# RMS norms of the second block: the next GEMM on x times gain, with rstd rows multiplied into its results

## The chip, the cores and the metric

One core of a Trainium2 chip runs the kernel. The metric is the device time of one execution, in microseconds. Its engines run side by side and meet only at semaphores: TensorE (PE) for matmuls, VectorE (DVE) and ScalarE (ACT) for elementwise work, GpSimd (POOL), and SyncE (SP), which here only issues DMAs.

## What is computed

The reference is two transformer-like blocks on x of 512 tokens by 1024 features, in float32. The change touches the second one. What matters of it:

```python
h = rmsnorm(x, g_mix)                       # x * rsqrt(mean(x*x) + eps) * gain
proj = h @ w_in                             # 11 parts of 1024 columns
xc, gb, gc, q, k, v, g_sw, gate_a, gate_r = split(proj)
u = gc * xc
conv = three taps over the tokens of u      # each feature for itself
y_a = (gb * conv) @ w_a_out
...                                         # retention over q, k, v -> y_r
x = x + (sigmoid(gate_a) * y_a + sigmoid(gate_r) * y_r) @ w_o
h2 = rmsnorm(x, g_ffn)
x = x + (silu(h2 @ w_ff_gate) * (h2 @ w_ff_up)) @ w_ff_down
return rmsnorm(x, g_final)
```

The rstd of a token multiplies a whole column of the transposed h, so `(x * gain * rstd) @ w` is `(x * gain) @ w` with each token's results times its rstd. For u = gc * xc that is rstd squared.

## The kernel before

Everything is kept transposed: 128 features on the partitions, the 512 tokens along the row, 8 such k-tiles for 1024 features. A GEMM is made of units. A unit is 128 output features: the weight slab of 128 x 1024 is loaded by SP (`load`, four slots), split on ACT into `w_hi` (`act_convert`, L380) and on DVE into the rest `w_lo` (`dve_convert`, L385), two units ahead (`AHEAD = 2`). `pe_unit` (L368) then runs three passes of 8 matmuls: w_hi by the operand's hi, w_lo by its hi, w_hi by its lo. ACT takes the result out of PSUM (`act_out`, L392). The order on each engine is that of the program, one stream for each.

The stages of the second half, in order: output projection of block one (8 units, `U_WO`), convolution (24 units, `U_CONV`: the three columns xc, gc, gb of eight tiles, one turn t for each tile), `U_YA` (16), retention's q, k, v (32), gates (24), `U_YR` (16), `U_O` (8), feed-forward (`U_FF`, 44 units, gate and up of 22 tiles), `U_DOWN` (24). Most of them are hardware loops (`Fori`) of a few turns.

A norm stands between `U_WO` and `U_CONV`, and another between `U_O` and `U_FF`. In each of them: `residual` (L1187, L1197) adds x and sums the squares that `out_and_square` makes on ACT (L784); `norm_sums` on PE (L1669) sums them over the partitions; DVE makes the mean (`norm_ms`, L1201); POOL the power of -0.5 (L579); `rows_bc` on PE (L1449) lays rstd along the rows in PSUM bank 5; `norm` on DVE makes t = x * gain * rstd for eight tiles (L1208); `round_norm` on ACT rounds them to `g_hi` (or `f_hi`, L789); DVE makes the rest `g_lo` (`f_lo`, L1212). Only then is the operand of the next GEMM there. Behind the first norm DVE also computes the retention's log decay, some thirty operations on 8 columns (L1222 to L1248), with one Exp on ACT (L798) in between. In the convolution, DVE multiplies xc by gc, applies three taps (L1263, L1265, L1268), multiplies by gb (L1273); ACT rounds to `a_hi` (L808), DVE makes `a_lo` (L1275).

Of the kernel before, what the change touches and what calls it, by code (L numbers as in the profile page):

```python
# [25 lines left out]
F32 = mybir.dt.float32  # L26
# [131 lines left out]
def hybrid_block(nc, x, c, w_ada, b_ada, norm_gain, w_in, b_nsa_gate, q_gain_a, k_gain_a, sinks,  # L158
# [7 lines left out]
    with ExitStack() as stack:  # L166
# [15 lines left out]
        def const(name, shape, dt=F32):  # L182
# [97 lines left out]
        ret = sb("ret", [P, 16, S], R + 48)  # L280
        ret_hi = sb("ret_hi", [P, 16, S], R + 48, F32R)
# [29 lines left out]
        m_hi = sb("m_hi", [P, KT, S], R, F32R)  # L311
        m_lo = sb("m_lo", [P, KT, S], R + 16, F32R)
# [3 lines left out]
        t_f = sb("t_f", [P, KT, S], R + 48)  # L316
# [11 lines left out]
        raw_in2 = [sem(f"raw_in2_{s}") for s in range(SLOTS)]  # L328
# [4 lines left out]
                 "tab_in consts csilu_done col_t col_done x_tr x_ev sumsq_done line_mm line_ev "  # L333
# [12 lines left out]
        nrm = {n: sem(n) for n in ("x_done xsq_done ss_done nst_mm ms_done rs_done nbc_mm t_done h_done l_done").split()}  # L346
# [9 lines left out]
        def pe_unit(pe, it, per, u, per_o, o, mov_hi, mov_lo, kts=KT, k0=0, first=True, last=True,  # L356
                    hi_sem=None, lo_sem=None, base=0):
# [6 lines left out]
            for n, (w, mov, ready) in enumerate(passes):  # L364
                for k in range(kts):
                    if ready is not None:
                        pe.wait_ge(ready, base + k0 + k + 1)
                    mm = pe.matmul(bank, w[:, slot, k], mov[:, k0 + k],  # L368
                                   start=first and n == 0 and k == 0,
                                   stop=last and n == 2 and k == kts - 1)  # L370
            mm.then_inc(unit_done, 1)

        def act_convert(act, it, per, u, kts=KT):
            slot = u % SLOTS
            act.wait_ge(raw_in[slot], at(it, 4 * per, 16 * (u // SLOTS + 1)))
            if u < U_PAIRED:
                act.wait_ge(raw_in2[slot], at(it, 4 * per, 16 * (u // SLOTS + 1)))
# [22 lines left out]
        def tile_of(t, it, per, n):  # L400
# [3 lines left out]
            return t[:, bass.ds(it * per + n, 1)].rearrange("p a n -> p (a n)")  # L404

# [18 lines left out]
        def _(sp):  # L424
# [17 lines left out]
            def load_pair(u, dst, dst2, src, src2):  # L442
# [4 lines left out]
                sp.dma_start(dst2, src2).then_inc(raw_in2[u % SLOTS], 16)  # L447
# [30 lines left out]
            with sp.Fori(0, 2) as it:  # L478
                for k in range(4):
                    load(it, 4, U_WO + k, w_out_v[:, :, wide(it * 512 + k * P)])  # L480
            with sp.Fori(0, 2) as it:
                for t in range(4):
                    for n, off in enumerate((0, 2048, 1024)):
                        load(it, 12, U_CONV + 3 * t + n, w_in2_v[:, :, wide(it * 512 + off + t * P)])
# [23 lines left out]
            with sp.Fori(0, 2) as it:  # L508
                for k in range(4):
                    load(it, 4, U_O + k, w_o_v[:, :, wide(it * 512 + k * P)])  # L510
            with sp.Fori(0, FT // 2) as it:
                for t in range(2):
                    load(it, 4, U_FF + 2 * t, w_g_v[:, :, wide(it * 256 + t * P)])
                    load(it, 4, U_FF + 2 * t + 1, w_u_v[:, :, wide(it * 256 + t * P)])
# [13 lines left out]
        def _(pool):  # L528
# [93 lines left out]
            pool.wait_ge(nrm["t_done"], KT)  # L622
# [37 lines left out]
        def _(act):  # L660
# [29 lines left out]
            with act.Fori(0, 2) as it:  # L690
                for k in range(8, 12):
                    act_convert(act, it, 4, k + AHEAD)
                    act_out(act, it, 4, k, tile_of(proj, it, 4, k), k, ACT.Copy)

            def square(t):
# [6 lines left out]
            for n in range(16, 24):  # L702
# [17 lines left out]
                if n < 19:  # L720
                    for t in range(*NORM_GROUPS[n - 16]):
                        square(t)
# [55 lines left out]
            def out_and_square(it, per, u, per_o, o, q, t, scale):  # L778

                act_out(act, it, per, u, t[:, o % 2], o, ACT.Copy, scale)  # L780
                count = at(it, per_o, q * KT + o - NORM_O[q] + 1)
                apart(act, it)
                act.wait_ge(nrm["x_done"], count)
                a.activation(t[:, 2 + o % 2], tile_of(x_t, it, per_o, o - NORM_O[q]), ACT.Square).then_inc(nrm["xsq_done"], 1)  # L784

            def round_norm(q, dst, t):
                for k in range(KT):
                    act.wait_ge(nrm["t_done"], q * KT + k + 1)
                    a.activation(dst[:, k], t[:, k], ACT.Copy).then_inc(nrm["h_done"], 1)  # L789

            with act.Fori(0, 2) as it:
                for k in range(4):
# [1051 lines left out]
```

## Time and profile before

| | |
|---|---|
| time, median of 3 runs | 1593.28 us (1589.33, 1593.28, 1594.75) |
| span of the profiled execution, first to last instruction | 1585.1 us (its own whole time is not recorded; the median is 8.2 us above the span) |
| PE matmul busy | 1515.8 us, 96% |
| DVE busy | 704.2 us, 44% |
| ACT busy | 589.0 us, 37% |
| POOL busy | 92.0 us, 6% |
| mean granted PE clock | 0.973 of full speed |
| DMA | 147.87 MB, mean 93 GB/s |

How to read it: the busy time of PE is an average over stages, and a busy PE is not always PE at full clock. A timeline row gives start, duration, engine, line, operation, tile written and tiles read, and in brackets how long the engine had been idle and what ended it. Matmuls overlap, so the end of a row is a little later than the start of the next; the distance between two starts is the time that counts.

### The profile page before, as it was taken

The page shows a single profiled execution, that of the slowest core. Times are in us where ns is not written, and L with a number is a line of the kernel's source. Part 1 is how long each engine was busy: PE and PEld are TensorE (multiplying, and loading weights), DVE is VectorE, ACT ScalarE, POOL GpSimd, SP SyncE. Part 2 cuts the span into 40 slices and gives each one's busy share as a digit, 9 for nine tenths or more (in the row PEclk, how much of TensorE's full clock was granted, in tenths as well). Part 3 has the DMA queues.
Part 4 walks back from the last instruction along what each step waited for, and adds up shares of the span by engine and source line. Part 5 has one row for each costly group of instructions (what it writes and reads, how often), then busy time and mean ns, then how long its engine had stood idle before and what let it go on. Part 6 is the DMA issues. An engine that isn't in the chain of part 4 may idle for free.

```text
span 1585.1 us, 20029 instructions
## 1 busy us (share of the span) xinstructions
PE 1515.8 (96%) x7068; PEld 1247.0 (79%) x7068; DVE 704.2 (44%) x1078; ACT 589.0 (37%) x955; POOL 92.0 (6%) x97
## 2 busy tenths in 40 slices
PE   7799998998989999999999999999998999999997
PEld 4578886887768888887787878887876888888886
DVE  4443256764465442344453524454445333333332
ACT  5232335653433334333333344443333333332321
POOL 5100500000000000000000023210000000000000
PEclk9799899998989999999999999999998999999999
DMA  9963320000333333331121213325232333333321
GB/s 328 328 135 95 106 60 9 1 2 14 89 134 89 100 97 102 93 94 53 53 80 52 79 54 93 93 80 157 82 96 63 106 93 93 105 92 99 99 84 53
DMA packets 243191, 147.87 MB, mean 93 GB/s; under 512 B 21490, under 2 KB 237758, under 8 KB 241732
## 3 DMA queue, kind: packets, MB, share of 16 engines
q1 hardware_dynamic: 239652, 131.63, 28.5%
q0 software_dynamic: 3488, 15.58, 2.9%
q8 instruction: 29, 0.48, 0.1%
q14 instruction: 22, 0.18, 0.0%
HBM read 138.81 MB, written 7.34 MB: 92 GB/s over the span
## 4 chain that ended last, share of the span: by engine, by line
PE 67%; issue 25%; DMA 3%; DVE 2%; ACT 2%; POOL 0%; DVEq 0%; POOLq 0%; SPq 0%; ACTq 0%
PE ps L368 50%; PE ps L1449 3%; PE ps L1731 3%; PE ps L1627 3%; PE ps L1641 2%; DMA w_raw<-in_w_in_dram 2%; PE ps L1708 1%; PE ps L1471 1%; PE ps L1526 1%; DMA bias_line<-bias_lines 1%; PE ps L1519 1%; DVE ret_val L1386 0%; PE ps L1615 0%; DMA rel_bias_sb<-in_rel_bias_dram 0%; PE ps L1494 0%
## 5 line engine op out<-in xcount | busy, mean ns | idle before, releaser
L385 DVE TENSOR_TENSOR w_lo<-w_raw,w_hi 128x1024 fp32r<-128x1024 f32 (+1 forms) x221 | 268.2, 1218 | 324.5 <-ACT w_hi L380 320.7
L380 ACT ACTIVATE w_hi<-w_raw 128x1024 fp32r<-128x1024 f32 (+1 forms) x221 | 228.9, 1043 | 32.4 <-DMA w_raw<-in_w_in_dram 18.8
L368 PE MATMUL ps<-g_hi,w_hi 128*128 128x512 f32 x704 | 181.0, 399 | 1.9 <-ACT g_hi L789 1.6
L368 PE MATMUL ps<-g_hi,w_lo 128*128 128x512 f32 x704 | 175.6, 392 | 0.0
L368 PE MATMUL ps<-g_lo,w_hi 128*128 128x512 f32 x704 | 174.1, 390 | 0.0
L368 PEld LDWEIGHTS ps<-g_hi,w_hi 128*128 128x128 f32 x704 | 131.8, 189 | 33.5 <-issue 4.9
L368 PEld LDWEIGHTS ps<-g_hi,w_lo 128*128 128x128 f32 x704 | 133.3, 189 | 28.1
L368 PEld LDWEIGHTS ps<-g_lo,w_hi 128*128 128x128 f32 x704 | 132.5, 188 | 27.6
L392 ACT ACTIVATE temps<-ps 128x512 f32<-128x512 f32 x68 | 40.7, 598 | 262.2 <-PE ps L368 262.2
L368 PE MATMUL ps<-f_hi,w_hi 128*128 128x512 f32 x352 | 90.3, 398 | 1.6 <-ACT f_hi L789 1.6
L368 PE MATMUL ps<-f_hi,w_lo 128*128 128x512 f32 x352 | 88.6, 395 | 0.0
L368 PE MATMUL ps<-f_lo,w_hi 128*128 128x512 f32 x352 | 87.0, 389 | 0.0
L368 PEld LDWEIGHTS ps<-f_hi,w_hi 128*128 128x128 f32 x352 | 66.9, 190 | 17.9 <-ACT f_hi L789 2.5
L368 PEld LDWEIGHTS ps<-f_hi,w_lo 128*128 128x128 f32 x352 | 67.2, 191 | 14.1
L368 PEld LDWEIGHTS ps<-f_lo,w_hi 128*128 128x128 f32 x352 | 66.2, 188 | 13.9
L1641 PEld LDWEIGHTS ps<-proj,probs_t 128*128 128x128 f32 x432 | 61.5, 192 | 13.9 <-issue 7.6
L757 ACT ACTIVATE scores_sb<-scores_sb,row_min 128x256 f32<-128x256 f32 (+3 forms) x96 | 51.2, 533 | 54.2 <-DVE row_min L1122 53.3
L368 PE MATMUL ps<-h_hi,w_hi 128*128 128x512 f32 x200 | 58.4, 439 | 11.9 <-issue 10.6
L1641 PE MATMUL ps<-proj,probs_t 128*128 128x64 f32 x432 | 58.6, 263 | 0.0
L368 PEld LDWEIGHTS ps<-h_hi,w_hi 128*128 128x128 f32 x200 | 40.7, 209 | 22.2 <-issue 12.1
L579 POOL TENSOR_TENSOR rstd<-mean_squares,minus_half 128x4 f32<-128x4 f32 x8 | 10.2, 1276 | 777.9 <-DVE mean_squares L1201 743.6
L1627 PE MATMUL ps<-proj 128*128 128x256 f32 (+3 forms) x160 | 53.9, 418 | 0.0
(329 smaller groups left out, 2141.7 us busy)
## 6 DMA issues: line engine op xcount, KB each, us to landing
w_raw<-in_w_in_dram SPq DMA_DIRECT2D x95, 512.0 KB, 3.9
w_raw<-in_w_ff_gate_dram SPq DMA_DIRECT2D x22, 512.0 KB, 3.8
w_raw<-in_w_ff_up_dram SPq DMA_DIRECT2D x22, 512.0 KB, 3.7
w_raw<-in_w_in_dram SPq DMA_DIRECT2D x36, 256.0 KB, 4.3
w_ada_shift_scale<-in_w_ada_dram SPq DMA_DIRECT2D x8, 1024.0 KB, 20.2
w_raw<-in_w_r_out_dram SPq DMA_DIRECT2D x16, 512.0 KB, 4.3
w_raw<-in_w_ff_down_dram SPq DMA_DIRECT2D x16, 512.0 KB, 4.2
w_ada_gate<-in_w_ada_dram SPq DMA_DIRECT2D x2, 2048.0 KB, 12.9
```

The source lines that it names most:

```text
L368: mm = pe.matmul(bank, w[:, slot, k], mov[:, k0 + k], start=first and n == 0 and k == 0, stop=last and n == 2 and k == kts - 1)
L380: act.activation(whi[:, slot, 0:kts], raw[:, slot, 0:kts], ACT.Copy).then_inc(hi_done, 1)
L385: nc.vector.tensor_tensor(wlo[:, slot, 0:kts], raw[:, slot, 0:kts], whi[:, slot, 0:kts].bitcast(F32), ALU.subtract).then_inc(lo_done, 1)
L392: act.activation(dst, ps[:, o % 4], func, scale=scale).then_inc(evac, 1)
L757: a.activation(sc[:, s % 2, 0:w], sc[:, s % 2, 0:w], ACT.Exp, scale=-1.0, bias=row_min[:, G % 2, n:n + 1], accum_out=den[:, G % 2, att(s). ...
L1449: return pe.transpose(dst, src, ident[0:parts, 0:parts])
L1471: pe.matmul(ps[:, 4 + h % 3, 0:LINE], rel[:, h:h + 1].to_broadcast([33, P]), onehot[:, h // 8], start=True, stop=True).then_inc(m["line_mm ...
L1519: mm = pe.matmul(ps[:, 4, 8 * t + 2 * i:8 * t + 2 * i + 2], proj[:, 20 + t % 4, blk(i)], half_sel[:], start=True, stop=True)
L1526: mm = pe.matmul(ps[:, 7, c0 + 64 * c:c0 + 64 * c + 64], w1[:, q, blk(c)], xp[:, q].rearrange("p g n -> p (g n)"), start=q == 0, stop=q == ...
L1627: pe.matmul(ps[:, s % 2, 0:u.width], proj[:, q, blk(u.i)], keys[:, u.first_block * P:u.first_block * P + u.width], start=True, stop=True). ...
L1641: mm = pe.matmul(ps[:, 4 + u.group % 2, u.head * HD:(u.head + 1) * HD], pt[:, t % 2, blk(b)], proj[:, v, c:c + HD], start=b == 0, stop=b = ...
L1731: mm = pe.matmul(ps[:, PV_BANK[t]], w[:, j, blk(t)], p[:, j], start=n == 0 and j == 0, stop=n == 2 and j == NI - 1)
```

## The change

Both norms are made the same way:

- In the GEMM before the norm, ACT also rounds x * gain to `x_gain_hi` (or `x_ffn_hi`) and DVE makes the rest, per tile, as soon as the tile of x is there.
- The next GEMM's units run on that operand: all 24 of the convolution, the first 8 of the feed-forward part. Unit 0 runs its k-tiles 0 to 6 in all three passes and then k-tile 7 (`last_apart`). The column sums stand behind unit 0, the rstd rows behind unit 1.
- ACT copies the rows and their squares to SBUF (`rstd_rows`). DVE multiplies results by them: u by rstd squared, conv by rstd; gate and up of four tiles by rstd, with Silu on ACT as an instruction of its own behind that.
- The normalised operand (`g_hi`, `g_lo`, `f_hi`, `f_lo`) is made beside this, one tile a turn in the convolution, two a turn in the first four turns of the feed-forward stage. PE waits for all of it before `U_YA`, and before feed-forward unit 8.
- The log decay is computed in turn 2 of the convolution.
- The loops of the stages concerned, and those of units 8 to 15, are written out. The paired loads count on one semaphore. Tiles are placed anew, and feed-forward tiles 0 to 3 go to the end of `act_hi` (`act_at`). The spill of x waits for x only.

The core of the diff:

```diff
     def pe_unit(..., base=0, last_apart=False, hi_at=None):
+            for ks in (range(kts - 1), range(kts - 1, kts)) if last_apart else (range(kts),):
+                for n, (w, mov, ready) in enumerate(passes):
+                    for k in ks:
...
 # PE
-            norm(0, tt)
-            with pe.Fori(0, 2) as it:
-                for k in range(12):
-                    pe_unit(pe, it, 12, U_CONV + k, 12, O_CONV + k, g_hi, g_lo,
-                            hi_sem=nrm["h_done"] if k == 0 else None, lo_sem=nrm["l_done"] if k == 0 else None)
+            for k in range(3 * KT):
+                pe_unit(pe, None, 0, U_CONV + k, 0, O_CONV + k, xg_hi, xg_lo, hi_sem=nrm["xh_done"] if k == 0 else None,
+                        lo_sem=nrm["xl_done"] if k == 0 else None, last_apart=k == 0)
+                if k == 0:
+                    norm_sums(0, tt)
+                if k == 1:
+                    norm_rows(0)
+
+            pe.wait_ge(nrm["l_done"], KT)
...
+            for k in range(2 * FT):
+                hi, lo = (xf_hi, xf_lo) if k < 8 else (f_hi, f_lo)
+                if k == 8:
+                    pe.wait_ge(nrm["l_done"], 2 * KT)
...
 # ACT
+            def rows_out(q):
+                act.wait_ge(nrm["nbc_mm"], q + 1)
+                a.activation(rb[:, 0], ps[:, 5], ACT.Copy).then_inc(nrm["rb_done"], 1)
+                a.activation(rb[:, 1], ps[:, 5], ACT.Square).then_inc(nrm["rb_done"], 1)
+            for t in range(KT):
+                for n in range(3):
+                    act_convert(act, None, 0, U_CONV + 3 * t + n + AHEAD)
+                    act_out(act, None, 0, U_CONV + 3 * t + n, conv_ev[:, t % 2, n], O_CONV + 3 * t + n, ACT.Copy)
+                    if t == 0 and n == 1:
+                        rows_out(0)
+                round_norm(0, t, g_hi, t_n)
+                if t == 2:
+                    act.wait_ge(m["lgt_done"], 1)
+                    a.activation(lt[:, 1], lt[:, 0], ACT.Exp, scale=-1.0).then_inc(m["lgexp_done"], 1)
+                act.wait_ge(m["af_done"], t + 1)
+                a.activation(a_hi[:, t], tt[:, t % 2], ACT.Copy).then_inc(m["ah_done"], 1)
 # DVE, a turn of the convolution
+                dve_convert(dve, None, 0, U_CONV + 3 * t + AHEAD)
+                if t == 0:
+                    norm_ms(0)
+                dve_convert(dve, None, 0, U_CONV + 3 * t + 1 + AHEAD)
+                norm_tile(0, t, V_MIX, t_n)
+                dve.wait_ge(evac, O_CONV + 3 * t + 2)
+                own(v.tensor_tensor(conv_t[:], ev[:, 0], ev[:, 1], ALU.mult))
+                own(v.tensor_tensor(u_pad[:, 1:S + 1], conv_t[:], rb[:, 1], ALU.mult))
...
+                norm_rest(0, t, t_n, g_lo, g_hi)
+                dve_convert(dve, None, 0, U_CONV + 3 * t + 2 + AHEAD)
+                if t == 2:
+                    log_decay()
+                own(v.tensor_tensor(conv_t[:], conv_t[:], rb[:, 0], ALU.mult))
+                v.tensor_tensor(tt[:, t % 2], conv_t[:], ev[:, 2], ALU.mult).then_inc(m["af_done"], 1)
 # DVE, a turn t < 4 of the feed-forward stage, behind its two conversions
+                    norm_tile(1, 2 * t, V_FFN, t_f)
+                    norm_tile(1, 2 * t + 1, V_FFN, t_f)
+                    v.tensor_tensor(tt[:, t % 2], tt[:, t % 2], rb[:, 0], ALU.mult).then_inc(m["gate_done"], 1)
+                    own(v.tensor_tensor(tt[:, 2 + t % 2], tt[:, 2 + t % 2], rb[:, 0], ALU.mult))
+                    norm_rest(1, 2 * t, t_f, f_lo, f_hi)
+                    norm_rest(1, 2 * t + 1, t_f, f_lo, f_hi)
+                    dve.wait_ge(m["silu_done"], t + 1)
 # POOL
-            pool.wait_ge(nrm["t_done"], KT)
+            pool.wait_ge(nrm["x_done"], KT)
             pool.dma_start(x1_dram, x_t[:]).then_inc(m["spill_done"], 16)
```

## Rows read from the trace of the kernel before

**Rows 1.** The page, busy us, share of the span and instructions.

```profile
PE 1515.8 (96%) x7068; PEld 1247.0 (79%) x7068; DVE 704.2 (44%) x1078; ACT 589.0 (37%) x955; POOL 92.0 (6%) x97
```

**Rows 2.** Timeline around the first norm: start, us, engine, line, operation, count [idle before].

```profile
431.88 1.97 PE L368 MATMUL ps<-y_lo,w_hi 128*128 128x512 f32 x8
...
434.82 0.69 DVE L1187 TENSOR_TENSOR x_t<-temps,x_t 128x512 f32 x1 [1.78 <-ACT temps L392]
...
437.05 1.37 PE L1669 MATMUL ps<-ones,temps 128*128 128x1 f32 x8 [3.20 <-DVE temps L1197]
...
442.46 5.31 PE L368 MATMUL ps<-g_hi,w_hi 128*128 128x512 f32 x8 [1.59 <-ACT g_hi L789]
...
452.96 1.98 PE L368 MATMUL ps<-g_hi,w_hi 128*128 128x512 f32 x8
```

**Rows 3.** Timeline around the second norm, PE.

```profile
1196.67 1.98 PE L368 MATMUL ps<-m_lo,w_hi 128*128 128x512 f32 x8
...
1217.72 1.98 PE L368 MATMUL ps<-f_hi,w_hi 128*128 128x512 f32 x8
```

**Rows 4.** Stretches: A:B us, busy (x) PE PEld DVE ACT POOL, PEclk, DMA.

```profile
437.60:437.80 0.20, 0.20 (x3) 0.20 (x3) 0.00 (x0) 0.00 (x0) 0.00 (x0) 0.54 0.00 0
...
450.80:451.00 0.20, 0.20 (x2) 0.10 (x2) 0.20 (x2) 0.00 (x0) 0.00 (x0) 0.50 1.93 819
...
847.20:847.40 0.20, 0.20 (x1) 0.20 (x2) 0.20 (x1) 0.00 (x0) 0.00 (x0) 0.54 0.00 0
```

**Rows 5.** Timeline of PE in the gate stage: column sums and rstd rows between units.

```profile
946.85 0.94 PE L1494 MATMUL ps<-ones,head_ssq 128*128 128x1 f32 x8
947.66 2.11 PE L368 MATMUL ps<-g_hi,w_hi 128*128 128x512 f32 x8
...
958.68 0.60 PE L1449 MATMUL ps<-ident,rstd 128*128 128x128 f32 x4
959.03 2.09 PE L368 MATMUL ps<-g_hi,w_hi 128*128 128x512 f32 x8
```

**Rows 6.** Timeline of one turn of the convolution stage, from a unit boundary.

```profile
464.10 1.98 PE L368 MATMUL ps<-g_hi,w_hi 128*128 128x512 f32 x8
464.30 0.60 ACT L392 ACTIVATE conv_evac<-ps 128x512 f32<-128x512 f32 x1 [4.15 <-PE ps L368]
465.02 0.69 DVE L1273 TENSOR_TENSOR temps<-conv_t,conv_evac 128x512 f32<-128x512 f32 x1 [1.37 <-ACT conv_evac L392]
465.84 0.63 ACT L808 ACTIVATE a_hi<-temps 128x512 f32 x1 [0.94 <-DVE temps L1273]
...
466.38 1.04 ACT L380 ACTIVATE w_hi<-w_raw 128x1024 fp32r<-128x1024 f32 x1
...
467.46 1.23 DVE L385 TENSOR_TENSOR w_lo<-w_raw,w_hi 128x1024 fp32r<-128x1024 f32 x1
```

**Rows 7.** Groups of DVE, 453 to 600: line, names, shapes, count, busy us, mean ns.

```profile
L1265 DVE SCALAR_TENSOR_TENSOR conv_t<-u_pad,columns,conv_t 128x512 f32<-128x512 f32 x8 | 6.0, 752 | 1.2 <-DVE conv_t L1263 0.3
```

**Rows 8.** Timeline of DVE, first and last of the log-decay operations.

```profile
451.00 0.16 DVE L1222 TENSOR_SCALAR log_decay_steps<-decay_logits 128x8 f32<-128x8 f32 x1
...
456.86 0.17 DVE L1248 TENSOR_SCALAR log_decay<-log_decay 128x4 f32<-128x4 f32 x1
```

**Rows 9.** Waits of PE (us in total, times, longest); critical chain (start, us, what).

```profile
PE ps L1731 <- ACT p_hi L820: 7.9, 4, 2.0
...
719.07 10.50 PE ps L1731 x45
...
847.14 12.09 PE ps L1731 x45
```

**Rows 10.** Critical chain: eight units written out, six units from a loop.

```profile
101.75 43.70 PE ps L368 x192
...
859.23 32.64 PE ps L368 x144
```

**Rows 11.** Timeline of ACT, the last table load of the kernel.

```profile
1048.62 1.28 ACT L392 ACT_TABLE_LOAD   x1
```

More of the change, by code:

```diff
@@ L476, in wide @@
                 return bass.ds(n, P)
[L478 to L484, printed above, removed]
+            for k in range(KT):
+                load(None, 0, U_WO + k, w_out_v[:, :, k * P:(k + 1) * P])
+            for t in range(KT):
+                for n, off in enumerate((0, 2048, 1024)):
+                    load(None, 0, U_CONV + 3 * t + n, w_in2_v[:, :, off + t * P:off + (t + 1) * P])
             with sp.Fori(0, 4) as it:
@@ L507, in _ @@
                     load(it, 8, U_YR + k, w_yr_v[:, 8 * half:8 * half + 8, wide(it * 512 + (k // 2) * P)])
[L508 to L514, printed above, removed]
+            for k in range(KT):
+                load(None, 0, U_O + k, w_o_v[:, :, k * P:(k + 1) * P])
+            for t in range(FT):
+                load(None, 0, U_FF + 2 * t, w_g_v[:, :, t * P:(t + 1) * P])
+                load(None, 0, U_FF + 2 * t + 1, w_u_v[:, :, t * P:(t + 1) * P])
             with sp.Fori(0, 2) as it:
@@ L689, in _, with square_head @@
                 act_out(act, None, 0, n, proj[:, n], n, ACT.Copy)
[L690 to L695, printed above, removed]
+            for k in range(8, 16):
+                act_convert(act, None, 0, k + AHEAD)
+                act_out(act, None, 0, k, proj[:, k], k, ACT.Copy)
+            def square_head(t):
                 if t >= 4:
@@ new lines, in _ @@
+            for k in range(KT):
+                act_convert(act, None, 0, U_WO + k + AHEAD)
+                act_out(act, None, 0, U_WO + k, tt[:, (O_WO + k) % 2], O_WO + k, ACT.Copy, mod[:, 16 + k:17 + k])
+                gain_round(0, k, V_MIX, xg_hi)
+                square(0, k, tt, O_WO + k)
+            for t in range(KT):
+                for n in range(3):
[9 more added lines that the diff above has]
+                a.activation(a_hi[:, t], tt[:, t % 2], ACT.Copy).then_inc(m["ah_done"], 1)
@@ L1220, in _ @@
-            norm(0, V_MIX, t_g, g_lo, g_hi)
-            own(v.tensor_scalar(lt[:, 0], decay[:], -1.0, None, ALU.mult))
-            own.wait()
-            own(v.tensor_tensor(lt[:, 0], lt[:, 0], decay[:], ALU.max))
-            own.wait()
-            v.tensor_copy(lt[:, 4], lt[:, 0]).then_inc(m["lgt_done"], 1)
-            dve.wait_ge(m["lgexp_done"], 1)
-            own(v.tensor_scalar(lt[:, 2], lt[:, 1], 2.0, None, ALU.add))
-            own.wait()
-            own(v.reciprocal(lt[:, 2], lt[:, 2]))
@@ L1231, in _ @@
-            own.wait()
-            own(v.tensor_tensor(lt[:, 2], lt[:, 2], lt[:, 1], ALU.mult))
-            own.wait()
-            own(v.tensor_tensor(lt[:, 3], lt[:, 2], lt[:, 2], ALU.mult))
-            own(v.memset(lg[:], 1.0 / 19))
-            own.wait()
-            for n in range(17, -1, -2):
-                own(v.tensor_tensor(lg[:], lg[:], lt[:, 3], ALU.mult))
+            for k in range(KT):
+                dve_convert(dve, None, 0, U_WO + k + AHEAD)
+                residual(O_WO + k, 0, tt, x_t, lo=(V_MIX, xg_hi, xg_lo))
@@ new lines, in log_decay @@
+                own(v.tensor_tensor(lt[:, 3], lt[:, 2], lt[:, 2], ALU.mult))
+                own(v.memset(lg[:], 1.0 / 19))
+                own.wait()
+                for n in range(17, -1, -2):
+                    own(v.tensor_tensor(lg[:], lg[:], lt[:, 3], ALU.mult))
+                    own.wait()
+                    own(v.tensor_scalar(lg[:], lg[:], 1.0 / n, None, ALU.add))
+                    own.wait()
+                own(v.tensor_tensor(lg[:], lg[:], lt[:, 2], ALU.mult))
+                own(v.tensor_scalar(lt[:, 1], decay[:], 0.0, None, ALU.min))
```

317 lines of the change are left out of this document (155 added, 162 removed).

## The prediction

> **What bounds the kernel now.** I read the page first. TensorE (PE) is busy for 1515.8 of 1585.1 us [rows 1], so an edit is worth only what it gives back of the other 69 us, and of stretches in which PE is busy at half clock. Then I looked for these stretches around the two norms that the change touches, in the timeline by engine. In the first, the last GEMM pass before the norm starts at 431.88 and the second GEMM unit behind it at 452.96: 21.08 us [rows 2]. What the GEMMs need of that at full clock is one pass of 8 matmuls (1.81 us) and one unit of 24 (5.44 us, from six units in 32.64 us [rows 10]). The reader should see the chain in these rows: the ScalarE (ACT) eviction, x_t on VectorE (DVE) at 434.82, its square on ACT, column sums on PE at 437.05, the rstd rows, and then a unit that starts at 442.46 but is fed one k-tile at a time. The second norm has the same picture: 1196.67 to 1217.72, 21.05 us [rows 3]. Part of it is clock: the granted clock falls at about 437.7, after PE had nothing from 433.85, and is still 0.50 (the 1.2 GHz level) at 451 [rows 4].
>
> **What the change takes away.** With x times gain as operand, unit 0 of the next GEMM needs no rstd. Its first 21 matmuls need k-tiles 0 to 6, which exist. The last k-tile is ready after x_t's end (435.51), a hand-over of 0.13, a rounding of 0.63 on ACT, another hand-over, and its low part (0.75, the DVE operation with two tensors and a column [rows 7]): about 437.2. PE asks for it at 433.7 plus 21 x 0.227, so 438.4: covered by 1.2 us; were that cover gone, it would cost what is missing, one for one. The conversions of the weights shift by 0.6 us on ACT and 0.8 on DVE per unit in the GEMM before; they run two units (10.9 us) ahead, so this costs nothing.
>
> What stays of the norm on PE is the column sums behind unit 0 and the rstd rows behind unit 1. The trace shows both kinds between units at full clock, in the gate stage: the sums from 946.85 to 947.66 and a next pass that is longer (2.11 for 1.98), so 0.94; the rows from 958.68 to 959.03 and 2.09 for 1.98, so 0.46 [rows 5]. Their inputs come long before (the sum of squares at about 438 for 439.1, rstd some 1.5 us after the sums and a unit ahead of its use). So a norm falls from 21.08 to 1.81 + 5.44 + 0.94 + 0.46 = 8.65: minus 12.4 us. Two norms: minus 24.8.
>
> **What it puts in their place.** Behind the GEMM start, DVE and ACT now do the norm's work per tile, in program order with the weight conversions, and PE waits where that order is late. I laid the new order out with the hand-overs of one turn of the conv stage [rows 6]: PE's unit boundary at 464.10, eviction 0.20 later and 0.60 long (the next on ACT starts 0.50 later), DVE 0.12 after its end, 0.69 per product, ACT 0.13 after that, 0.63 long (the next 0.54 after its start), a weight conversion of 1.05 on ACT and one of 1.23 on DVE 0.04 behind it. T is the unit boundary at which a turn's third unit ends.
> - Conv stage, ordinary turn: eviction to 0.80, g_hi rounded to 1.33, g_lo on DVE to 2.15, w_lo of unit 3t+4 to 3.42 (PE wants it at 5.44), the two products to 5.0, a_hi to 5.75, w_hi of 3t+5 to 6.7, its w_lo to 8.0 (PE wants it at 10.88). No stall; 2.9 us are left.
> - Turn t = 2 also holds the log-decay steps on DVE, ahead of the products. In the trace they run from 451.00 to 457.03, 6.0 us [rows 8], beside units of PE that had what they needed. Now ACT's conversion for unit 11 is queued behind af_done, which is behind these 6.0 us, and PE waits for it: 8.0 + 6.0 = 14.0 for 10.88, so plus 3.2 us.
> - At the end of the stage PE waits for all of g_lo before the next stage's unit. g_lo[7] is made at T + 2.15, after the last unit: plus 2.3 us.
> - Feed-forward stage: its first four turns (8 units) are on the raw operand, and unit 8 waits for all of f_lo. A turn of the chain, from one scaling of the gate to the next, is 0.69 + 0.13, Silu 0.54, two roundings 0.54 + 0.63, 0.13, f_lo 0.69, product 0.73, 0.13, act_hi 0.54, w_hi 1.05, eviction 0.50, w_hi 1.05, w_lo 1.27, two tiles of x times gain times rstd 1.52: 10.1 to 10.3 us, just under the 10.88 that PE takes for two units. It starts 3.5 us after unit 1 ends (the rows to 0.6, two evictions of them to 1.8, two tiles). So the fourth turn's scaling is at 3.5 + 3 x 10.3 = 34.4, and f_lo[7] another 3.4 later, at 37.8 to 38; PE is ready at 0.46 + 6 x 5.44 = 33.1. Plus 4.9 us.
> - Covered, at nothing: the extra evictions, products and squares elsewhere (DVE is idle 6 of 16 us of a conv turn); the earlier spill of x on GpSimd's queue (10 us sooner, behind the two table loads as before, with weights loaded four units ahead); the merged semaphores; the other order of the activation tiles, which changes addresses only.
>
> New waits: 3.2 + 2.3 + 4.9 = 10.4. Net before the clock: 24.8 - 10.4 = 14.4 us less.
>
> **The clock.** Each new wait may let the clock fall. The nearest rows are four waits of 1.97 us for p_hi. In three the PV matmuls behind took 10.50 us; in the fourth the clock fell as the wait ended and they took 12.09: a fall costs 1.6 us, and a wait of 2 us brings it one time in four [rows 4, 9]. In the other direction, 3.2 us of nothing followed by the small column sums brought it both times [rows 2, 4]. The most that one fall could cost is half of the stretch that PE then works at 0.50: from 442.46 to 451, so 4.2 us; the least is 0. I take the nearest row, 1.6, for the waits of 3.2 and 4.9 us, and nothing for that of 2.3: 3.2 us. The Trainium skill (TensorE: Matmul & The Clock Gate, "HAM oscillation") says that bursts with waits between them start again at the low clock each time, which speaks against trading one long idle stretch for three shorter ones. By it all three waits would pay, 4.8 us for my 3.2; the one in four of the p_hi rows agrees only in part.
>
> **The sum.** 14.4 - 3.2 = 11.2 us less. The profiled span of 1585.1 becomes 1573.9. No run's whole time stands beside that span; the median of the runs is 8.2 us above it, launch and end, which the change doesn't touch. 1593.3 - 11.2 = **1582.1 us**.
>
> **The rivals.**
> - Lighter waits, no fall or one (the chain is a little faster, the phases are kind): up to 14.4 us and the spread of the runs, 1577 to 1580. For it: the three p_hi waits without a fall. Chance 0.22.
> - Heavier: three falls, one at the 4.2 us end, or a chain of the feed-forward turns that is longer than 10.88, from where on each 0.1 us of a turn is paid by PE: minus 5 to 8 us, 1585 to 1588.5. Chance 0.12.
> - No change: Silu now runs in its own instruction between copies. If each needed the function table changed and changed back, a raw turn would have 2 x 1.28 us more (a load's time [rows 11]), 10.3 us over four turns, all ahead of unit 8: 1592. Against it: in the feed-forward stage of before, Silu and copies alternate and the kernel's last table load is at 1048.62, before that stage [rows 11]. Or all falls at 4.2 us, 12.6 for 3.2: 1591.5. The Trainium skill (ScalarE: Activation LUTs, "Table sets") has copy in every set, which would mean no load either, and leaves the chance as it is. Chance 0.09.
> - Slower: the loops are written out. 92 units (8 + 8 + 24 + 8 + 44) that PE, ACT and DVE ran from loops become straight code. If the instruction stream then lagged, each unit would pay, and from 0.17 us per unit on (14.4 + 1.6 over 92) the kernel is slower than before; at 0.25, 1605. Against it: eight units that were straight code took 43.70 us, 5.46 each, looped ones 5.44 [rows 10]: 1.8 us over 92. Chance 0.04.
> - That the change doesn't do what it says (the first unit does not start at once) needs the last k-tile to be late by more than 1.2 us, and costs no more than what is missing: it is within the heavier case.
>
> **How the numbers follow.** Forecast 0.53, lighter 0.22, heavier 0.12, no change 0.09, slower 0.04. The three first are all faster by over 0.3% (4.8 us, about what a measurement of this kernel can tell from no change): 0.87. Within it 0.09, slower 0.04. The range goes from the light end, 14.4 and the 2 us by which runs of one kernel differ, 1577, to the heavy end, 1589.5, which leaves out the slower case and most of no change.
>
> **What the profile of the changed kernel would show.** PE goes on at 433.9 without a gap, with sums and rows between units, and the granted clock stays 1.00 there. The waits table has three new entries of PE: for w_hi or w_lo once in the conv stage (about 3.2), for g_lo (2.3) and for f_lo (4.9). ACT and DVE do no more table loads than before. I am wrong if PE waits in every turn of a stage, if the units in straight code are longer than 5.46, or if the clock stays low for longer behind the new waits.

## The result and the profile after

| | before | after |
|---|---|---|
| median | 1591.3 us (4 runs, 1587.63 to 1594.75) | 1574.51 us (4 runs, 1574.13 to 1577.15) |
| ratio to before | | 0.9902 (95%: 0.988 to 0.9924) |
| whole time of the profiled execution | not recorded | 1574.43 us |
| its span | 1585.1 us | 1572.7 us |
| mean granted PE clock | 0.973 | 0.981 |

The forecast was 1582.1 us with a range from 1577.0: the time lies 7.6 us under the first and 2.5 us under the second. The forecast of the span was 1573.9 and the span is 1572.7. So most of the miss lies in the step from the span to the whole time, and 1.2 us of it in the working on the trace; the experiments first settle this, then the terms.

The page of the changed kernel, busy time, share and instructions, answers to [rows 1]:

```profile
PE 1508.2 (96%) x7068; PEld 1244.6 (79%) x7068; DVE 731.3 (46%) x1118; ACT 600.3 (38%) x979; POOL 92.1 (6%) x97
```

The number of matmuls is the same. PE's busy time fell by 7.6 us though the span fell by 12.4: the rest was idle time. DVE has 27 us and ACT 11 us more to do.

Timeline of PE around the first norm and then the second, answering to [rows 2, 3] (columns as there):

```profile
431.66 1.98 PE L374 MATMUL ps<-y_lo,w_hi 128*128 128x512 f32 x8
433.47 1.75 PE L374 MATMUL ps<-x_gain_hi,w_hi 128*128 128x512 f32 x7
...
438.23 0.39 PE L374 MATMUL ps<-x_gain_hi,w_hi 128*128 128x512 f32 x1
...
438.91 0.95 PE L1710 MATMUL ps<-ones,temps 128*128 128x1 f32 x8
439.72 2.11 PE L374 MATMUL ps<-x_gain_hi,w_hi 128*128 128x512 f32 x8
...
445.31 0.60 PE L1491 MATMUL ps<-ident,rstd 128*128 128x128 f32 x4
445.66 2.09 PE L374 MATMUL ps<-x_gain_hi,w_hi 128*128 128x512 f32 x8
```

```profile
1199.83 0.95 PE L1710 MATMUL ps<-ones,temps_o 128*128 128x1 f32 x8
1200.63 2.11 PE L374 MATMUL ps<-x_ffn_hi,w_hi 128*128 128x512 f32 x8
...
1206.22 0.60 PE L1491 MATMUL ps<-ident,rstd 128*128 128x128 f32 x4
```

There is no gap. From the last pass of the old GEMM to unit 1 it is 439.72 - 431.66 = 8.06 us, plus 0.35 and 0.11 for the rows behind unit 1: 8.5 where 21.08 stood. The row at 438.23 is the k-tile that comes last, run apart.

The new waits of PE, from the table of waits (us in total, times, longest) and then from its timeline, where the bracket is the idle time ahead of the row. The wait in the convolution stage has "issue" in its bracket: the profile finds nothing that ended it. That it belongs to the log decay is shown further down, by the rows of DVE and ACT and by two experiments.

```profile
PE ps L374 <- DVE f_lo L1239: 3.1, 1, 3.1
...
PE ps L374 <- DVE g_lo L1239: 2.3, 1, 2.3
```

```profile
492.92 1.98 PE L374 MATMUL ps<-x_gain_lo,w_hi 128*128 128x512 f32 x8
497.45 2.83 PE L374 MATMUL ps<-x_gain_hi,w_hi 128*128 128x512 f32 x7 [2.56 <-issue]
```

```profile
568.07 1.97 PE L374 MATMUL ps<-x_gain_lo,w_hi 128*128 128x512 f32 x8
572.37 3.17 PE L374 MATMUL ps<-g_hi,w_hi 128*128 128x512 f32 x8 [2.33 <-DVE g_lo L1239]
```

```profile
1237.51 1.98 PE L374 MATMUL ps<-x_ffn_lo,w_hi 128*128 128x512 f32 x8
...
1242.54 3.48 PE L374 MATMUL ps<-f_hi,w_hi 128*128 128x512 f32 x8 [3.05 <-DVE f_lo L1239]
```

A pass takes 1.81 us, so the three waits cost 497.45 - 494.73 = 2.72, 572.37 - 569.88 = 2.49 and 1242.54 - 1239.32 = 3.22 us. The first pass behind each should show 1.98 and shows 2.83 (for seven matmuls), 3.17 and 3.48: PE is at half clock. The restart alone is a small part of this: behind the same wait with no fall a pass of eight shows 2.09 to 2.11 for 1.98 (two rows further down). The stretches of time around them, with the granted clock (columns as in [rows 4]):

```profile
499.00:501.00 2.00, 2.00 (x7) 1.52 (x6) 1.93 (x4) 0.00 (x0) 0.00 (x0) 0.50 0.89 264
574.00:576.00 2.00, 2.00 (x6) 1.58 (x5) 1.14 (x2) 1.50 (x2) 0.09 (x1) 0.50 0.74 222
1243.00:1244.00 1.00, 1.00 (x4) 0.72 (x4) 0.30 (x2) 0.88 (x2) 0.00 (x0) 0.50 0.00 0
433.00:497.00 64.00, 61.89 (x279) 51.02 (x277) 38.99 (x77) 22.11 (x33) 2.66 (x4) 1.00 0.39 124
1194.00:1239.00 45.00, 45.00 (x206) 37.38 (x205) 29.47 (x39) 21.18 (x32) 1.03 (x1) 1.00 0.33 96
```

Ahead of the waits, across both norms, the clock is 1.00 (last two rows).

### The profile page after: what moved, and what is told of

Read it like the earlier page. It is cut to its first block, busy times and chain, and to the rows that moved or that the text cites. A ratio compares the mean times of both kernels' runs of the same rounds, so it can differ in the third digit from the quotient of the medians.

```text
span 1572.7 us, 19027 instructions
## 1 busy us (share of the span) xinstructions
PE 1508.2 (96%) x7068; PEld 1244.6 (79%) x7068; DVE 731.3 (46%) x1118; ACT 600.3 (38%) x979; POOL 92.1 (6%) x97
## 4 chain that ended last, share of the span: by engine, by line
PE 66%; issue 25%; DMA 4%; DVE 2%; ACT 1%; SPq 0%; POOL 0%; POOLq 0%; DVEq 0%; ACTq 0%
PE ps L374 51%; PE ps L1491 3%; PE ps L1773 3%; PE ps L1668 3%; PE ps L1682 2%; DMA w_raw<-in_w_in_dram 2%; DMA w_ada_shift_scale<-in_w_ada_dram 2%; PE ps L1750 1%; PE ps L1567 1%; DMA bias_line<-bias_lines 1%; PE ps L1560 1%; DVE ret_val L1418 0%; PE ps L1656 0%; PE ps L1536 0%; DVE ada_sum L950 0%
## 5 line engine op out<-in xcount | busy, mean ns | idle before, releaser
L374 PE MATMUL ps<-g_hi,w_hi 128*128 128x512 f32 x512 | 131.3, 399 | 2.6 <-DVE g_lo L1239 2.3
L374 PE MATMUL ps<-g_hi,w_lo 128*128 128x512 f32 x512 | 127.1, 391 | 0.0
L374 PE MATMUL ps<-g_lo,w_hi 128*128 128x512 f32 x512 | 126.5, 389 | 0.0
L374 PEld LDWEIGHTS ps<-g_hi,w_hi 128*128 128x128 f32 x512 | 95.5, 189 | 24.5 <-issue 5.3
L374 PEld LDWEIGHTS ps<-g_hi,w_lo 128*128 128x128 f32 x512 | 96.7, 189 | 20.5
L374 PEld LDWEIGHTS ps<-g_lo,w_hi 128*128 128x128 f32 x512 | 96.1, 188 | 19.9
L374 PE MATMUL ps<-f_hi,w_hi 128*128 128x512 f32 x288 | 72.6, 395 | 3.1 <-DVE f_lo L1239 3.1
L374 PE MATMUL ps<-f_lo,w_hi 128*128 128x512 f32 x288 | 71.1, 389 | 0.0
L374 PE MATMUL ps<-f_hi,w_lo 128*128 128x512 f32 x288 | 71.1, 389 | 0.0
L374 PEld LDWEIGHTS ps<-f_hi,w_lo 128*128 128x128 f32 x288 | 54.1, 188 | 11.2
L374 PEld LDWEIGHTS ps<-f_lo,w_hi 128*128 128x128 f32 x288 | 54.1, 188 | 11.2
L588 POOL TENSOR_TENSOR rstd<-mean_squares,minus_half 128x4 f32<-128x4 f32 x8 | 10.3, 1285 | 772.1 <-DVE mean_squares L1226 737.5
```

The lines of the kernel that those rows point to most:

```text
L374: mm = pe.matmul(bank, w[:, slot, k], mov[:, at_k], start=first and n == 0 and k == 0, stop=last and n == 2 and k == kts - 1)
```

## The experiments

Each kernel ran beside the kernel before on the same chip, in three groups. In the first (first four below) the kernel before had a median of 1588.56 us over 21 runs, in the second (the next four) 1589.15 over 9, in the third (the last two) 1588.51 over 9. The time of a stretch is the distance between the first matmuls of its stages in the profile. I use CONV to YA1 (unit 0 of the convolution to the first unit on `a_hi`: 25 units) and FF to DOWN (44 units).

### How long the kernel before is

No edit: the kernel before as it stands.

> The kernel before, unchanged, to see how its own executions spread and with what clock. Theory A (the profiled execution of before was a light one): spans from 1585 to 1593, the longer ones at a lower granted clock, and the whole time 1.5 to 2 us above the span each time, so that the 8.2 us by which the median stood above the profiled span was not launch but a longer execution. Rival B (the sum missed a gain of 4 to 5 us): spans all within 2 us of 1585, whole times 6 to 8 us above them.

Median 1587.9 us (11 runs, 1586.16 to 1594.0), ratio 0.9987 (0.9974 to 1.0). This time each profiled execution had its whole time beside it. That of the profile shown here was 1594.0 us at a span of 1592.2, two others 1587.01 at 1585.3 and 1586.16 at 1584.4. In all executions of this study for which both are on record the whole time is 1.7 to 2.2 us above the span, never 8.2. So the profiled execution of before, span 1585.1, had a whole time of about 1587, and two of the three runs behind the median of 1593.28 were long ones. Over all 54 runs of the kernel before in this study the median is 1588.6 us, and 11 of them are above 1591. So the execution with the span of 1585.1 was some 1.6 us lighter than the middle one, and the median of three 4.7 us heavier. The forecast of this run, long executions at a lower granted clock, held for the longest only: those from 1592.98 us on have 0.969 or 0.970 where their clock is on record, but the two at 1591.9 and 1592.06 have 0.975, like the short ones (0.972 to 0.978). What lengthened those two is open.

What made this one execution long is in its profile. Timeline of PE in the compression, in the kernel before (its long execution) and in the changed kernel:

```profile
151.70 11.56 PE L1526 MATMUL ps<-cmp_in,w_cmp 128*128 128x64 f32 x64 [0.68 <-DVE cmp_in L1001]
```

```profile
151.34 7.33 PE L1567 MATMUL ps<-cmp_in,w_cmp 128*128 128x64 f32 x64 [0.57 <-DVE cmp_in L1022]
```

The same 64 small matmuls take 11.56 us instead of 7.33. Stretches of the long execution:

```profile
150.00:160.00 10.00, 9.32 (x55) 8.85 (x54) 3.98 (x5) 1.54 (x2) 0.00 (x0) 0.71 0.37 102
160.00:170.00 10.00, 10.00 (x37) 8.54 (x37) 0.00 (x0) 2.35 (x5) 3.26 (x5) 0.61 0.43 143
```

The granted clock is 0.71 and 0.61 (in the profile of before the same two stretches have 1.00 and 0.90). The small matmuls and the GEMM unit behind them account for 4.2 and 2.3 us. In the other eleven profiles of this study the 64 matmuls take 7.33 us. What brings the fall is not known: PE's rows just ahead of it are alike, with 0.68 us of idle time in the profile of before too. The row of matmuls (L1615) that starts at 246.43 us in the profile of before starts at 253.06 in this one: it is 6.6 us late some 180 us ahead of the first changed norm. The second place is the PV matmuls behind the waits for `p_hi` [rows 9], here from the chain of waits of this execution, with two falls in four (the other two took 10.50 and 10.49 us):

```profile
788.63 12.13 PE ps L1731 x45
...
918.32 12.09 PE ps L1731 x45
```

### The changed kernel once more

No edit: the changed kernel as it stands.

> The changed kernel, unchanged, beside it. Theory A: the ratio to before comes out at 0.989 to 0.992 again by the medians, while the lightest execution of each differ by only 11 to 13 us; spans spread by 3 us or less. Rival B: the lightest executions differ by 16 to 17 us like the medians.

Median 1576.77 us (5 runs, 1574.85 to 1578.28), ratio 0.9921 (0.9906 to 0.9936). With the 9 runs of both measurements the changed kernel is at 1576.6, which is 12.0 us under the 1588.6 of before. The forecast of the difference was 11.2. The lightest executions of this group differ by 11.3 us, as expected of a base that was too heavy; the spans of the five runs spread by 3.4 us, a little more than the 3 expected.

### The kernel before without loops

```diff
-            with pe.Fori(0, 2) as it:          # and so on ACT, DVE, SP, in the stages concerned
+            for it in range(2):
```

> The kernel before with only the loops of these stages written out as straight code; norms as before. Theory A: PE does not notice, unit distance 5.44 us, time within 1.5 us of before; the hand-overs between ACT and DVE at the norms get 0.1 us shorter each since the waits are on constants, together under 1 us. Rival B (the hidden gain sits in the written-out loops): 3 to 5 us less. Rival C (straight code is slower): 0.02 to 0.25 us per unit more, 2 us or more in total.

Median 1586.77 us (11 runs, 1581.1 to 1589.45), ratio 0.9989 (0.9978 to 1.0001); CONV to YA1 141.07 us (before 141.32), FF to DOWN 243.92 (before 244.31). The two stages are 0.6 us shorter together. The times alone leave room for up to 3.5 us less, but not for a cost of 2 us: so straight code that is slower (rival C, and the prediction's "slower") is out by the times, and a hidden gain of 3 to 5 us (rival B) by the stages, of which this is one profiled execution. The loops do change one small thing, the hand-overs. Timeline around the boundary that [rows 6] show:

```profile
464.67 0.69 DVE L1275 TENSOR_TENSOR temps<-conv_t,conv_evac 128x512 f32<-128x512 f32 x1 [1.52 <-ACT conv_evac L392]
465.40 0.63 ACT L810 ACTIVATE a_hi<-temps 128x512 fp32r<-128x512 f32 x1 [0.76 <-DVE temps L1275]
...
466.06 0.69 DVE L1277 TENSOR_TENSOR a_lo<-temps,a_hi 128x512 fp32r<-128x512 f32 x1 [0.70 <-ACT a_hi L810]
```

DVE ends at 465.36 and ACT starts at 465.40; ACT ends at 466.03 and DVE starts at 466.06: 0.03 to 0.04 us each. In [rows 6] the same hand-over from DVE to ACT takes 0.13 (465.71 to 465.84).

### Only the first norm changed

The second norm as before: its rows ahead of unit 0, all feed-forward units on `f_hi` and `f_lo`.

```diff
-                hi, lo = (xf_hi, xf_lo) if k < 8 else (f_hi, f_lo)
-                if k == 8:
-                    pe.wait_ge(nrm["l_done"], 2 * KT)
+            norm_sums(1, tt_o)
+            norm_rows(1)                       # then the 44 units, on f_hi and f_lo
```

> The changed kernel with the second norm put back to the old way (feed-forward stage entirely on the normalised operand, all made before unit 0; its own loops stay written out). Only the second norm's gain should go. From the traces PE's distance from the second norm's last pass to the same place behind unit 8 got 7.7 us shorter, so theory A says 7 to 8 us more than the changed kernel, that is 4 to 6 us less than before by lightest executions. Rival B with a gain spread over the stages: less than 6 us more.

Median 1581.74 us (5 runs, 1581.25 to 1582.9), ratio 0.9952 (0.9939 to 0.9966). From the first unit of `U_O` to DOWN it takes 298.18 us where the changed kernel takes 290.83: the second norm gives 7.35 us, as expected. By the medians it gives 5.1 (against all nine runs of the changed kernel), by the shortest runs 7.1. The medians alone would fit the rival (a gain spread over the stages, under 6 us); it is the stages that speak against it. CONV to YA1 is 146.08 us, the 146.05 of the changed kernel: the first half keeps its time without the second.

### PE waits for each tile, not for all

```diff
-            pe.wait_ge(nrm["l_done"], KT)
-                    pe_unit(pe, it, 4, U_YA + 2 * t, 4, O_YA + 2 * t, g_hi, g_lo)
+                    pe_unit(pe, it, 4, U_YA + 2 * t, 4, O_YA + 2 * t, g_hi, g_lo,
+                            hi_sem=nrm["h_done"] if t == 0 else None, lo_sem=nrm["l_done"] if t == 0 else None)
...
-                if k == 8:
-                    pe.wait_ge(nrm["l_done"], 2 * KT)
-                pe_unit(..., hi_sem=nrm["xh_done"] if k == 0 else None, ...)
+                pe_unit(..., hi_sem={0: nrm["xh_done"], 8: nrm["h_done"]}.get(k), ...)
```

> The changed kernel, but PE does not wait for all of the normalised operand before the first unit that uses it; it waits per k-tile (hi in the first pass, rest in the third). The profile of the changed kernel shows g_hi[7] rounded 1.3 us behind the unit boundary (571.19 for 569.88) and used 1.6 us behind it, f_hi[7] 2.4 us behind (1241.68 for 1239.32) and used 1.6 us behind. My theory (each wait costs what its last tile lacks, plus a fall of the clock of 1.6): the wait for g_lo (2.5 us) and its fall go, the wait for f_lo shrinks from 3.2 to 0.8 us and its fall goes: 5 to 8 us less than the changed kernel. Rival (the falls cost nothing extra, the waits are all): 4.9 us less. Rival (the operands would be waited for elsewhere, at the third pass): under 3 us less.

Median 1565.51 us (5 runs, 1564.51 to 1566.76), ratio 0.9844 (0.983 to 0.9859). Timeline of PE where the two waits were:

```profile
568.35 1.98 PE L374 MATMUL ps<-x_gain_lo,w_hi 128*128 128x512 f32 x8
570.16 1.98 PE L374 MATMUL ps<-g_hi,w_hi 128*128 128x512 f32 x8
```

```profile
1235.43 1.52 PE L374 MATMUL ps<-f_hi,w_hi 128*128 128x512 f32 x6
1237.32 1.02 PE L374 MATMUL ps<-f_hi,w_hi 128*128 128x512 f32 x2 [0.37 <-ACT f_hi L804]
1238.18 2.00 PE L374 MATMUL ps<-f_hi,w_lo 128*128 128x512 f32 x8
```

The wait for `g_lo` is gone. In place of that for `f_lo` PE runs six matmuls and then waits for the seventh tile of `f_hi` (0.37 us idle by the profile; from start to start the pass takes 2.75 us for 1.81, so it costs 0.94), and the next pass is at full clock (2.00 us, at 1238.18). CONV to YA1 is 141.89 us (4.16 less: the wait of 2.49 and its fall of 1.7), FF to DOWN 241.74 (3.77 less), 7.9 together. The medians differ by 11, more than the stages show and more than the 5 to 8 expected. The profiled execution was the longest of its five (1566.76), that of the changed kernel one of its shortest; the rest isn't settled.

### The log decay in pieces

The thirty operations as six pieces, one each in turns 1 to 6, ACT's Exp in turn 1.

```diff
-                if t == 2:
-                    log_decay()
+                if 1 <= t <= 6:
+                    next(pieces, None)
```

> The changed kernel, with the log decay cut in six pieces of about 1 us, one in each of the turns 1 to 6, where 2.9 us of a turn were left. Theory: the wait of PE for unit 11's weights (2.7 us in the profile) and the fall of the clock behind it go, 2.7 to 4.3 us less than the changed kernel, no wait in any other turn. Rival (the wait comes from the extra products of DVE, not the log decay): no change or pieces of the wait in several turns.

Median 1569.55 us (4 runs, 1568.41 to 1572.56), ratio 0.987 (0.9853 to 0.9887): 7.1 us under the changed kernel, where 2.7 to 4.3 were expected. The two stages show 4.6 of it (6.0 less and 1.4 more); the rest isn't settled. CONV to YA1 is 140.05 us, 6.0 less. Gone are the wait of 2.7 and its fall, with no wait in any other turn (so it was the log decay, not the added products of DVE), and the fall behind `g_lo`, which did not come this time though the wait did:

```profile
567.57 2.11 PE L374 MATMUL ps<-g_hi,w_hi 128*128 128x512 f32 x8 [2.32 <-DVE g_lo L1239]
569.51 1.99 PE L374 MATMUL ps<-g_hi,w_lo 128*128 128x512 f32 x8
```

2.11 us behind a wait of 2.32, where the changed kernel had 3.17 behind 2.33. FF to DOWN was 246.91 us, 1.4 more than in the changed kernel, so the fall there cost 2.9 instead of 1.5. What decides whether a wait of this length brings a fall, and how long it lasts, these runs don't settle.

### The last k-tile with the others

```diff
-                        lo_sem=nrm["xl_done"] if k == 0 else None, last_apart=k == 0)
+                        lo_sem=nrm["xl_done"] if k == 0 else None, last_apart=False)
```

> The changed kernel, with unit 0 of both stages in the old order of k-tiles (three passes of eight, the last k-tile not kept apart). The first pass then needs the hi of k-tile 7 1.6 us after the start and it is ready 2.4 us after (435.84 for 433.47): PE should wait 0.8 to 0.9 us in each of the two norms, with no fall of the clock, 1.7 us more in total, at the edge of what can be measured; the trace should show both waits. Rival (apart order is what makes the whole change work): 5 us or more.

Median 1576.76 us (4 runs, 1571.59 to 1578.1), ratio 0.9912 (0.9888 to 0.9936). The waits are there, 0.68 and 0.59 us, the first here:

```profile
433.10 1.75 PE L374 MATMUL ps<-x_gain_hi,w_hi 128*128 128x512 f32 x7
435.52 0.50 PE L374 MATMUL ps<-x_gain_hi,w_hi 128*128 128x512 f32 x1 [0.68 <-ACT x_gain_hi L794]
```

Unit 0 with its sums takes 440.32 - 433.10 = 7.22 us for 6.25, and 7.14 for 6.25 at the second norm. So running the tile apart is worth 0.97 and 0.89 us, together 1.9 for the 1.7 expected, which the medians, 0.1 us apart, cannot show. One thing more stands in this profile: the wait behind the log decay, as long as in the changed kernel, brought no fall.

```profile
498.08 2.09 PE L374 MATMUL ps<-x_gain_hi,w_hi 128*128 128x512 f32 x8 [2.59 <-issue]
```

That is why CONV to YA1 is 145.52 us here, 0.5 less than in the changed kernel and not 1 more. The fall behind `f_lo` was again one of 2.9 us, and FF to DOWN is 247.77.

### All three together

Waits by tile, log decay in pieces, and in the raw turns of the feed-forward stage the roundings of `f_hi` and the rests `f_lo` ahead of the second result's work:

```diff
+                if raw_t and t:
+                    round_norm(1, 2 * t, f_hi, t_f)
+                    round_norm(1, 2 * t + 1, f_hi, t_f)
                 act_out(act, None, 0, U_FF + 2 * t + 1, tt[:, 2 + t % 2], O_FF + 2 * t + 1, ACT.Copy)
...
+                    norm_rest(1, 2 * t, t_f, f_lo, f_hi)
+                    norm_rest(1, 2 * t + 1, t_f, f_lo, f_hi)
                     dve.wait_ge(evac, O_FF + 2 * t + 2)
                     own(v.tensor_tensor(tt[:, 2 + t % 2], tt[:, 2 + t % 2], rb[:, 0], ALU.mult))
```

> The changed kernel with both edits, the waits per tile and the log decay in pieces, and in the feed-forward turns 1 to 3 the two roundings ahead of the second eviction. All three new waits (2.7, 2.5 and 3.2 us) and their falls should be gone: 8.4 us less without falls, 13 us with three of 1.6; 1562 to 1568 us by median, 20 to 26 us below the kernel before.

Median 1562.24 us (5 runs, 1561.06 to 1563.6), ratio 0.9829 (0.9814 to 0.9843): 26 us under before and 14.4 under the changed kernel. Stretches across both changed places:

```profile
431.00:590.00 159.00, 159.00 (x709) 131.74 (x708) 97.48 (x148) 61.08 (x83) 3.55 (x5) 1.00 0.38 113
1183.00:1250.00 67.00, 67.00 (x303) 55.56 (x302) 41.24 (x53) 32.07 (x47) 1.03 (x1) 1.00 0.33 95
```

PE has no idle time and full clock. CONV to YA1 is 137.42 us and FF to DOWN 240.78: 25 and 44 units of 5.44 with 1.40 for the sums and rows (137.4 and 240.8). So the raw operand, without its waits, costs PE nothing but these 1.4 us per norm. Against the waits by tile alone (241.74) the order on ACT and DVE in the raw turns is worth 0.96 us, the rest of the wait for `f_hi`.

### One wait put back at a time

To the kernel with all three, either the wait for all of `g_lo`, or the log decay whole in turn 2.

```diff
+            pe.wait_ge(nrm["l_done"], KT)      # lone_g_wait, ahead of U_YA
```

> The kernel with all three edits, in which PE again waits for all of g_lo before the unit after the convolution (2.5 us in the profile of the changed kernel) and waits nowhere else new. It prices one wait alone. If each wait always brings a fall of the clock, as all three did in the changed kernel's profile: 2.5 + 1.7 = 4.2 us more than the kernel with all three edits, and the third unit's passes at 0.50. If a fall comes only in some executions (the forecast had none here): 2.5 us more in some, 4.2 in others, the profile showing either.

> The kernel with all three edits, in which the log decay stands in turn 2 in one piece again. PE should wait 2.7 us for the weights of unit 11 (forecast 3.2), plus 1.6 to 1.7 with a fall: 2.7 to 4.4 us more than the kernel with all three edits. Rival: the wait of this turn spoils later turns too, then more than 5.

```profile
566.71 3.09 PE L374 MATMUL ps<-g_hi,w_hi 128*128 128x512 f32 x8 [2.43 <-DVE g_lo L1242]
```

```profile
495.21 3.49 PE L374 MATMUL ps<-x_gain_hi,w_hi 128*128 128x512 f32 x8 [2.60 <-issue]
```

The first is the wait for `g_lo` alone, the second that of the log decay alone. Both first passes are at half clock (3.09 and 3.49 us for 1.98). CONV to YA1 is 141.75 us for the first (4.33 more than with neither) and 141.77 for the second (4.35 more): 2.6 us of wait and 1.7 of clock for the first, 2.8 and 1.6 for the second, with 0.1 us of restart in each second number. Both are the case with a fall of what was expected, and the second spoils no later turn. Together they give 8.68, and the changed kernel has 146.05 - 137.42 = 8.63 in this stage: in these profiled executions each wait pays its own fall, in addition. The medians are 1564.7 (5 runs, 1563.47 to 1569.73) and 1564.85 us (4 runs, 1563.07 to 1567.33), 2.5 and 2.6 above that of all three, ratios 0.9851 (0.9833 to 0.987) and 0.9851 (0.9835 to 0.9868). They were not in one group with it, so the stages carry this, not the medians.

## Why the prediction was wrong, and what of it was right

**The base of the sum was wrong, by 6.3 us.** The step that failed reads "the median of the runs is 8.2 us above it, launch and end, which the change doesn't touch". The runs showed 1.7 to 2.2 us. The other 6 us were the difference between a light profiled execution and a median of three with two long ones (1.6 and 4.7 us from the middle of 54 runs). The same 11.2 us on about 1587 (span 1585.1 and 1.9) give 1575.8, where the changed kernel has 1574.5 to 1576.8. Seen from the medians, the miss of 7.6 us is 4.7 of base (1593.3 for 1588.6), 0.8 of the sum (12.0 less for 11.2) and 2.1 by which the first four runs of the changed kernel were lighter than all nine (1574.5 for 1576.6). On the base of 1588.6 the forecast would have been 1577.4. The sign was in plain sight: three runs with 1589.33 as the shortest, and an execution of which nothing but the span was known.

**The sum itself: 12.4 us by the two profiles, 11.2 forecast, from misses that nearly cancel.** All of it lies between the first unit of `U_WO` and YA1 (196.52 to 191.75 us) and between that of `U_O` and DOWN (298.50 to 290.83).

| term | forecast | measured |
|---|---|---|
| gap at the two norms | -24.8 | -25.9 |
| wait behind the log decay | 3.2 | 2.7 |
| wait for g_lo | 2.3 | 2.5 |
| wait for f_lo | 4.9 | 3.2 |
| clock | 3.2 (two falls of 1.6) | 4.9 (two of 1.7, one of 1.5) |
| sum | -11.2 | -12.4, with 0.2 of small ends |

- **The gap.** Measured on the kernel with all three, in which nothing else stands: 13.5 and 12.4 us less than in the profile of before. About 1 us of the first is that execution's own: in the long profile of before the stretch from `U_WO` to YA1 takes 195.57 us, not 196.52. The step of 8.65 us per norm held.
- **The covers.** The last k-tile's low part starts at 435.88 and takes 0.75 us, so it ends at 436.63, with 438.23 asked (the low part itself at 438.69): covered by 1.6 us for the 1.2 of the prediction. ACT makes 26 table loads in both profiles and none in the feed-forward stage, and the looped stage's 5.44 us per unit holds in straight code.
- **The log decay.** The mechanism is as laid out: the product behind the log decay is late, `a_hi` follows at 494.52, then the two halves of the weights, and the matmul at 497.45, when `w_lo` ends (497.35).

```profile
493.80 0.69 DVE L1308 TENSOR_TENSOR temps<-conv_t,conv_evac 128x512 f32<-128x512 f32 x1
495.05 1.04 ACT L389 ACTIVATE w_hi<-w_raw 128x1024 fp32r<-128x1024 f32 x1
496.13 1.22 DVE L394 TENSOR_TENSOR w_lo<-w_raw,w_hi 128x1024 fp32r<-128x1024 f32 x1 [0.26 <-ACT w_hi L389]
```

- **f_lo, the term that was mis-sized.** I had a turn of 10.1 to 10.3 us, started 3.5 us behind unit 1. The first starts 3.14 behind 1206.22, and the next two start 9.35 apart. The three hand-overs of my turn at 0.03 for 0.13 are 0.3 us of the difference. Much of the rest is that an operation starts some 0.08 us ahead of the end of the one before it on its engine (0.68 long, 0.60 apart in the rows below), which I counted for ACT but not for DVE.

```profile
1209.36 0.68 DVE L1461 TENSOR_TENSOR temps<-temps,rstd_rows 128x512 f32<-128x512 f32 x1
1209.96 0.68 DVE L1463 TENSOR_TENSOR temps<-temps,rstd_rows 128x512 f32<-128x512 f32 x1
...
1218.71 0.68 DVE L1461 TENSOR_TENSOR temps<-temps,rstd_rows 128x512 f32<-128x512 f32 x1
...
1228.06 0.68 DVE L1461 TENSOR_TENSOR temps<-temps,rstd_rows 128x512 f32<-128x512 f32 x1
```

  With a chain that fast it catches up with PE, and something else is late, which I had not looked for. The last rows ahead of the wait, DVE and ACT together:

```profile
1238.13 0.69 DVE L1461 TENSOR_TENSOR temps<-temps,rstd_rows 128x512 f32<-128x512 f32 x1
1239.52 0.60 ACT L401 ACTIVATE temps<-ps 128x512 f32<-128x512 f32 x1 [3.89 <-PE ps L374]
1240.02 0.62 ACT L915 ACTIVATE temps<-temps 128x512 f32<-128x512 f32 x1
...
1240.54 1.14 ACT L804 ACTIVATE f_hi<-t_f 128x512 fp32r<-128x512 f32 x2
1241.19 1.29 DVE L1239 TENSOR_TENSOR f_lo<-t_f,f_hi 128x512 fp32r<-128x512 f32 x2 [0.34 <-ACT f_hi L804]
```

  ACT had been idle for 3.89 us: it stood ahead of unit 7's eviction, with Silu and the roundings in program order behind it. They could not start before unit 7 had ended, so the wait is 3.2 us however fast the chain is. The kernel with all three moves these operations ahead of that eviction and waits by tile, and the wait is gone; by tile alone left 0.94 us of it.
- **The clock.** One fall more than I counted: that behind `g_lo`. I went by the `p_hi` rows, one in four for 1.97 us. Over the twelve profiles of this study (before, after and the ten experiments) the four `p_hi` waits of each brought a fall 18 times in 48, not one in four. The new waits, 2.5 to 3.2 us from start to start, brought one each time in the changed kernel's profile and 14 times in 16 over all profiles. The two without one are that for `g_lo` in the kernel with the log decay in pieces, and that behind the log decay in the kernel with the last k-tile in line. A fall with its restart cost 1.5 to 1.7 us, and 2.9 in two of the four cases behind `f_lo`. The Trainium skill (TensorE: Matmul & The Clock Gate, "HAM oscillation") describes bursts of matmuls with waits between them that start at the low clock each time. Its waits are longer than those for `g_lo` and behind the log decay, so that it promises a fall at each of these was my reading, not the page's. This trace has one at all three, and the 4.8 us of that reading was nearer to the 4.9 measured than my 3.2; over all profiles, and for the `p_hi` waits, "each time" holds only in part.

**The chances.** Faster by over 0.3% held, with 0.87 on it. The case that came is the forecast's own in its mechanism, with one fall more. The time came out below even the lighter case (1577 to 1580), and not for its reason, since falls were more, not fewer: that is the base. The range was built on the terms of the change, 5 us down, 2 of them for the spread of runs, and the base was off by 6. One figure of the slower case does not fit the sum: with 11.2 us to lose, 92 units lose them from 0.12 us per unit on, not 0.17. As the units in straight code took 5.44 us, nothing hung on it.

## What to carry to other kernels

Ahead of any sum, set the runs' times against the span of the profiled execution: where they differ by more than the constant between span and whole time, one of the two is an unusual execution, and the base belongs into the range. When work is moved into the background, look for the operation that it stands behind in program order on each engine, and wait for it by tile: here two waits for all, one block of thirty small operations and one order on ACT took 14 of the 26 us that were to be had by the medians, and were gone with edits of a few lines. Price a new wait of PE at its length plus its fall, 1.5 to 1.7 us here and twice 2.9 (14 of 16 waits of 2.5 to 3.2 us brought one), and add these up wait by wait.

## What the runs showed of the hardware

- Executions of one kernel on one chip differ by up to 8.4 us (the kernel before, 1586.16 to 1594.56 us in 32 runs). In the one long profile most of it is a fallen clock in a row of 64 small matmuls (11.56 us for 7.33) and in what follows it; the rest comes in steps of 1.6 us behind waits of 2 us.
- A hand-over between DVE and ACT takes 0.03 to 0.04 us where the code is written out, and 0.13 in the loop. The prediction used 0.13 for both. Whether it is the loop or the way in which the wait's count is given was not tried apart.
